# A hybrid decoder layer on one core: the merge's sums moved from GpSimd to VectorE, and four smaller moves in the order of loads and splits

## The reference

```python
h = _half_ffn(h, ffn1_pre_g, ffn1_w_gate, ffn1_w_up, ffn1_w_down, ffn1_post_g)
u = _rmsnorm(h, mix_pre_g)
c_q, c_kv, k_rope_raw, xb, yb, gate_mla, gate_lru = split(u @ w_in)
o_mla = _mla_branch(c_q, c_kv, k_rope_raw, ...)   # 8 heads, causal, then @ w_o_mla
o_lru = _rglru_branch(xb, yb, ...)                # conv, gated recurrence, then @ w_o_lru
merged = sigmoid(gate_mla) * o_mla + sigmoid(gate_lru) * o_lru
h = h + _rmsnorm(merged @ w_out, mix_post_g)
h = _half_ffn(h, ffn2_pre_g, ffn2_w_gate, ffn2_w_up, ffn2_w_down, ffn2_post_g)
```

## Time and profile before

| | |
|---|---|
| median of 3 runs | 2362.24 us (2359.62 to 2364.76) |
| profiled execution, its own time | 2362.34 us |
| its span in the trace | 2360.6 us |
| mean granted clock of TensorE | 0.975 of full |
| TensorE busy | 2217.9 us, 94% of the span |
| VectorE busy | 1242.3 us, 53% |
| ScalarE busy | 954.4 us, 40% |
| GpSimd busy | 350.7 us, 15% |

### The profile page before, as it was taken

The page is one execution under the profiler, slowest core; times in us unless marked ns, Lnnn a source line. Parts: engine busy times, 40 slices in busy tenths (PEclk is TensorE's granted clock), DMA queues, the critical chain, the costliest instruction groups (busy, mean ns, idle before and its releaser), DMA issues.

```text
span 2360.6 us, 26136 instructions
## 1 busy us (share of the span) xinstructions
PE 2217.9 (94%) x10101; PEld 1839.7 (78%) x10101; DVE 1242.3 (53%) x1596; ACT 954.4 (40%) x1529; POOL 350.7 (15%) x377
## 2 busy tenths in 40 slices
PE   4999999999998999999997888978699999999997
PEld 3888888888887888888986777856588888888886
DVE  7556655433636665212114887757755555543444
ACT  5333333332434767212324666434433333332332
POOL 5000000000402222000013555424300000000020
PEclk8999999999999999999998999989799999999999
DMA  3222222164442111223211002344122222235342
GB/s 116 72 72 64 80 71 72 56 215 149 134 136 65 52 50 47 72 76 115 69 36 36 8 10 80 121 166 165 62 72 63 72 63 73 71 125 194 109 152 89
DMA packets 198596, 209.48 MB, mean 89 GB/s; under 512 B 22277, under 2 KB 159562, under 8 KB 198474
## 3 DMA queue, kind: packets, MB, share of 16 engines
q1 hardware_dynamic: 198474, 207.81, 27.5%
HBM read 174.75 MB, written 32.51 MB: 88 GB/s over the span
## 4 chain that ended last, share of the span: by engine, by line
PE 83%; DVE 7%; POOL 3%; issue 3%; ACT 3%; DMA 1%; SPq 0%; POOLq 0%; ACTq 0%; DVEq 0%
PE ps L88 27%; PE ps L89 27%; PE ps L90 27%; DVE u_lo L98 1%; PE ps L1955 1%; PE ps L1987 1%; DVE w_lo L98 1%; POOL a_rot L1872 1%; ACT a_probs L1931 1%; PE ps L357 1%; DVE entry_y L342 1%; DVE ff_t L98 0%; DVE a_s L1921 0%; ACT entry_squares L282 0%; DVE a_pt L98 0%
## 5 line engine op out<-in xcount | busy, mean ns | idle before, releaser
L98 DVE TENSOR_TENSOR w_lo<-w_raw,w_hi 128x1024 fp32r<-128x1024 f32 (+3 forms) x169 | 205.1, 1217 | 282.2 <-ACT w_hi L94 281.8
L88 PE MATMUL ps<-ff_t,ff_w_hi 128*128 128x512 f32 x704 | 275.2, 391 | 15.8 <-DVE ff_t L98 15.8
L98 DVE TENSOR_TENSOR ff_w_lo<-ff_raw,ff_w_hi 128x512 fp32r<-128x512 f32 x264 | 182.9, 694 | 191.5 <-ACT ff_w_hi L94 191.3
L89 PE MATMUL ps<-ff_t,ff_w_hi 128*128 128x512 f32 x704 | 274.9, 390 | 0.0
L90 PE MATMUL ps<-ff_t,ff_w_lo 128*128 128x512 f32 x704 | 274.8, 390 | 0.0
L88 PE MATMUL ps<-w_hi,ff_hs 128*128 128x512 f32 x672 | 262.0, 390 | 6.4 <-DVE ff_hs L98 6.4
L90 PE MATMUL ps<-w_hi,ff_hs 128*128 128x512 f32 x672 | 261.5, 389 | 0.0
L89 PE MATMUL ps<-w_lo,ff_hs 128*128 128x512 f32 x672 | 261.4, 389 | 0.0
L94 ACT ACTIVATE w_hi<-w_raw 128x1024 fp32r<-128x1024 f32 (+3 forms) x169 | 169.7, 1009 | 187.4 <-PE ps L90 151.5
L94 ACT ACTIVATE ff_w_hi<-ff_raw 128x512 fp32r<-128x512 f32 x264 | 165.0, 628 | 184.5 <-PE ps L90 178.9
L88 PE MATMUL ps<-ff_b,ff_w_hi 128*128 128x512 f32 x528 | 207.8, 394 | 9.9 <-issue 8.3
(11 more groups left out here) (277 smaller groups left out, 4098.9 us busy)
## 6 DMA issues: line engine op xcount, KB each, us to landing
w_raw<-in_ffn_w_down_dram SPq DMA_DIRECT2D x88, 512.0 KB, 3.5
ff_raw<-in_ffn_w_gate_dram SPq DMA_DIRECT2D x44, 512.0 KB, 3.8
ff_raw<-in_ffn_w_up_dram SPq DMA_DIRECT2D x44, 512.0 KB, 3.9
w_raw<-in_w_in_dram SPq DMA_DIRECT2D x32, 512.0 KB, 3.9
w_raw<-in_w_out_dram SPq DMA_DIRECT2D x24, 512.0 KB, 4.2
spill_scratch<-ff_st SPq DMA_DIRECT2D x44, 256.0 KB, 2.9
ff_h<-spill_scratch SPq DMA_DIRECT2D x4, 2048.0 KB, 9.9
entry_x<-in_x_dram SPq DMA_DIRECT2D x8, 512.0 KB, 6.9
```

The lines of the kernel that those rows point to most:

```text
L88: pe.matmul(out, lh, rh, start=start, stop=False, skip_group_check=go_on)
L89: pe.matmul(out, lh, rl, start=False, stop=False, skip_group_check=go_on)
L98: return nc.vector.tensor_tensor(lo, src, as_f32(hi), ALU.subtract)
```

## The change

Four edits:

1. `am.add` runs on VectorE, right behind the product of the same block. Its wait for the landed transfers goes, since the product has made it.
2. SyncE issues w_out's load i = 7 ahead of the wait for the merge's end. Then come the norm's first gain and its first input row; the second gain stands behind load 8, and the other three input rows behind loads 9, 10 and 11.
3. The weights of the fourth head (`att.n_a[3]`) are loaded ahead of the rotary key's copies, and split in the attention's third step and no longer ahead of the first.
4. V tiles 4 and 5 are split ahead of the last tile's columns, and VectorE's `swap` comes behind `units[2]`.

```diff
--- before.py
+++ after.py
@@ -2122,11 +2122,10 @@
         dve.wait_ge(self.S["m_hi"], d + 1)
         split_lo(self.nc, self.c.u_lo[:, d, :], self.sum[:, d % 2, :], self.c.u_hi[:, d, :]).then_inc(self.S["m_split"], 1)
 
-    def add(self, pool, d):
-        pool.wait_ge(self.S["prod_done"], d + 1)
-        pool.wait_ge(self.landed[d % 5], 32 * (d // 5 + 1))
+    def add(self, dve, d):
+        dve.wait_ge(self.S["prod_done"], d + 1)
         x = self.sum[:, d % 2, :]
-        self.nc.gpsimd.tensor_tensor(x, x, self.other[d % 5], ALU.add).then_inc(self.S["add_done"], 1)
+        self.nc.vector.tensor_tensor(x, x, self.other[d % 5], ALU.add).then_inc(self.S["add_done"], 1)
 
     def branch_of(self, pe, d, chunks):
         c, att = self.c, self.att
@@ -2426,8 +2425,9 @@
                         lat.store(sp, 6)
                         lat.store(sp, 7)
                         break
+                w.load(sp, att.n_a[3])
                 att.key_rope_copy(sp)
-                for n in att.n_a[3:] + am.n[0:5]:
+                for n in att.n_a[4:] + am.n[0:5]:
                     w.load(sp, n)
                 for d in range(5):
                     am.load(sp, d)
@@ -2436,14 +2436,16 @@
                     am.load(sp, d)
                 for i in range(24):
                     w.load(sp, op.n[i // 8][i % 8])
-                    if i == 6:
+                    if i == 7:
                         sp.wait_ge(am.S["m_split"], DK)
                         sp.wait_ge(att.S["t_done"], HEADS * HEAD_PIECES)
                         sp.wait_ge(att.S["o_split"], 5)
                         gain(entry.post_gain, a["mix_post_g"][0])
+                        mid2.load(sp, 0)
+                    if i == 8:
                         gain(entry.pre_gain, a["ffn2_pre_g"][0])
-                        for t in range(4):
-                            mid2.load(sp, t)
+                    if i in (9, 10, 11):
+                        mid2.load(sp, i - 8)
                     if i == 13:
                         mid2.store(sp, 0)
                         mid2.store(sp, 1)
@@ -2564,19 +2566,19 @@
                 att.v_hi(act, 3)
                 att.rope_act(act, units[0])
                 att.unit_act(act, units[1])
+                att.v_hi(act, 4)
+                att.v_hi(act, 5)
                 lat.columns_hi(act, NT - 1)
-                for t in range(4, NT - 1):
-                    att.v_hi(act, t)
+                att.v_hi(act, 6)
                 att.unit_act(act, units[2])
                 att.v_last_hi(act)
                 att.unit_act(act, units[3])
                 att.rope_act(act, units[2])
                 att.key_rope_hi(act, 1)
                 w.hi(act, att.n_a[2])
-                w.hi(act, att.n_a[3])
                 for n in range(last_step + 2):
                     att.act_step(act, n)
-                    if n % HEAD_TILES == 2 and 0 < n // HEAD_TILES < HEADS:
+                    if n % HEAD_TILES == 2 and n // HEAD_TILES < HEADS:
                         w.hi(act, heads[n // HEAD_TILES + 3])
                 att.take(act, HEADS - 1, 1)
                 att.pair_hi(act, 3, half_of(1), 2 * HEADS)
@@ -2655,8 +2657,6 @@
                 att.rope_pool(pool, units[2])
                 for n in range(last_step):
                     att.pool_step(pool, n)
-                for d in range(DK):
-                    am.add(pool, d)
                 for g in range(1, 3):
                     for k in range(DK):
                         for s, q in out_steps(g, k):
@@ -2759,26 +2759,27 @@
                 att.v_lo(dve, 3)
                 att.rope_dve(dve, units[0])
                 att.unit_dve(dve, units[1])
+                att.v_lo(dve, 4)
+                att.v_lo(dve, 5)
                 lat.columns_lo(dve, NT - 1)
+                att.v_lo(dve, 6)
+                att.unit_dve(dve, units[2])
                 lat.swap(dve, 1)
-                for t in range(4, NT - 1):
-                    att.v_lo(dve, t)
-                att.unit_dve(dve, units[2])
                 att.v_lo(dve, NT - 1)
                 att.unit_dve(dve, units[3])
                 att.rope_dve(dve, units[2])
                 att.key_rope_lo(dve, 1)
                 w.lo(dve, att.n_a[2])
-                w.lo(dve, att.n_a[3])
                 for n in range(last_step + 2):
                     att.dve_step(dve, n)
-                    if n % HEAD_TILES == 2 and 0 < n // HEAD_TILES < HEADS:
+                    if n % HEAD_TILES == 2 and n // HEAD_TILES < HEADS:
                         w.lo(dve, heads[n // HEAD_TILES + 3])
                 att.add(dve, HEADS - 1, 1)
                 att.pair_lo(dve, 3, half_of(1), 5)
 
                 for d in range(DK):
                     am.product(dve, d)
+                    am.add(dve, d)
                     w.lo(dve, outs[d + 3])
                     if d > 0:
                         am.merged_lo(dve, d - 1)
```

## The result

| | before | after |
|---|---|---|
| median of 4 runs | 2362.30 us | 2341.34 us (2338.76 to 2343.29) |
| ratio, 95% interval | | 0.9911 (0.9894 to 0.9928) |
| profiled execution, its span | 2362.34, 2360.6 us | 2340.64, 2338.5 us |
| mean granted clock of TensorE | 0.975 | 0.982 |

The change takes 21.0 us off the kernel. 2336.6 us was forecast, with a range of 2331 to 2346, so the sign and the range held, and the forecast is 4.7 us too low. Run once more beside the experiments, the same program had a median of 2338.96 us against 2362.71: 23.8 us.

A forecast was written before the change was run, and what follows sets the result against it. Most of the chain is TensorE, so only stretches where it stands still can give time. Attention's start -10.2 and merge with output projection -15.5 sum to -25.7 us from 2362.34, giving 2336.6 us, range 2331 to 2346.

The forecast's parts named there:

- (a): Attention's start: V tiles split sooner; query unit at 1268.5 instead of 1271.12, VectorE begins on it 4.3 us earlier.
- (b): Attention's start: the later swap delays GpSimd's two rotary sums; third head's split at 1278.0, 1.3 us given back.
- rival 1: Attention's start: rotary chain and a dropping clock cost another 5 us, total 2341.8 us; chance 0.10.
- (c): Attention's start: fourth head's weights loaded earlier; first maximum at 1278.8 and exponential at 1279.9, 10.1 to 10.2 us sooner.
- (d): Attention's first scores: TensorE may keep the upper clock level; gain bounded at 2.5 us, taken as 0.
- rival 4: Attention's first steps: the clock stays up, total 2334 us; counted inside the main forecast's 0.82 chance.
- (e): Merge: sums on VectorE, u_lo 3.42 to 1.23 us, turn 5.3 to 4.3 or 4.9; TensorE waits 0.6 us at branch 3.
- (f): Output projection's start: the 2.70 us wait for the third chunk goes; last pair wanted at 1549.9.
- Rival 2: Merge: u_lo stays at 3.42 us, merge gives +1.5 instead of -15.5, total 2353.6 us; chance 0.05.
- (g): Output projection: last chunk's earlier load removes the 7.57 us wait; pair 13.2 us earlier, plus 2.3 us from full clock.
- (h): Output projection's second group: input rows and second gain between chunks 8 to 11 are covered; taken as 0, bounds 0 and 3 us.
- Rival 3: Output projection: loads and input rows queue at whole landing times, +7.9 us, total 2370.2 us; chance 0.02.

The follow-up runs named there:

- e7_only_loads: Kernel before with only the second edit (w_out load i = 7 issued ahead of gains and input rows): 2351.05 us, 0.9960 of before.
- e8: Kernel before with only the first edit (merge sums on VectorE instead of GpSimd): 2354.48 us, 0.9974 of before.
- e3: Changed kernel with the third edit undone (fourth head's weights loaded behind the key's copies, split ahead of the first maximum): 2348.38 us, 0.9939 of before.
- e4: Changed kernel with the fourth edit undone (V tiles 4 and 5 split behind the last columns and the swap): 2339.53 us, 0.9901 of before.
- e5: Changed kernel with VectorE's swap one place earlier, ahead of the second half's query unit: 2336.63 us, 0.9896 of before.
- e9: Changed kernel measured once more, as it is: 2338.96 us, 0.9902 of before.
- e1: Changed kernel with the first edit undone (merge sums back on GpSimd): 2347.00 us, 0.9929 of before.
- e6: Changed kernel with input rows 1 to 3 behind w_out loads 10, 11 and 12 instead of 9, 10 and 11: 2337.47 us, 0.9901 of before.

## Why the prediction held, and what it missed

(a) *V tiles.* The unit was put at 7.0 us after the last transposition, and it starts at 7.05. The 1.7 us of idle time came as 1.46, and the unit ran at full clock (0.227 us a pass from 1269.43 on). VectorE begins it at 1271.45, 9.4 us after the transposition, where 9.1 was forecast. What was not seen is that the kernel before is not always as slow here as in its one profile. Eight of the nine passes of its unit ran at half clock (1271.12 to 1274.52, about 0.43 us each); in e7_only_loads, with the same instructions up to here and 3.76 us of waiting, the clock came back within the unit's first pass. In e7 and e8 the exponential stands at 26.29 and 26.66, not at 28.05. Against these two the attention's part is worth 7.7 to 8.0 us. Of the other 1.4 to 1.8 us, 1.2 to 1.5 are the slower clock in that one profile (VectorE begins on the unit 13.45 us after the transposition, and 11.97 and 12.23 in e7 and e8); the rest is ScalarE's longer wait for the transfer (6.89 us against 6.62 and 6.73). Undone one at a time, the transfer is worth 7.5 us (e3) and V tiles with the swap 0.9 (e4).

(b) *The swap, 1.3 us given back: this term was mis-sized.* The swap came at 1273.61, the two GpSimd sums ended at 1277.36 and the third head's split began at 1279.37, 17.3 us after the transposition in place of the 16.5 forecast. With the swap early the exponential comes 1.9 us sooner (e5), so 1.9 us is what was given back, 0.6 more than the step had; 0.3 us came late from (a). The step let GpSimd's sum start where the swap ends, and it starts 0.43 us later (1274.30 to 1274.73); the rest is in the two sums, 2.63 us in place of 2.5. The error is of rival 1's kind, but that rival had another 5 us.

(c) *Head 4.* ScalarE waits for no transfer, and the maximum starts 0.85 us after the split, at 1280.22, sooner than the 1281 that was named as a sign of being wrong. The step has the exponential follow the maximum alone. What it left out is ScalarE's table load: it begins at 1279.41, ends at 1280.69, and the exponential starts 0.02 us behind it, also in e5, where the load waits 0.22 us for the split of the key's rotary part (1279.54 to 1280.82, exponential 1280.83). So by these rows a shorter `w_lo` of the third head on VectorE would alone gain nothing there. The displaced split, 0.56 us at 1286.57, cost nothing that can be seen: head 0 from its first exponential to the mask of step 8 took 18.2 us here and 19.3 in e9, against 19.0 and 19.2 in e7 and e8, which lack that split. TensorE was busy with the scores in front of it. The exponential was forecast 10.1 us sooner and came 9.4 sooner.

(d) *Clock, taken as 0.* The scores began at the upper level after 2.50 us of idle time (0.89 from 1280 to 1284), fell to 0.50 from 1284 to 1288 and were at 0.76 to 1292; before, 0.51 held from 1290 to 1302. From the first exponential to the mask of step 8 the head took 18.2 us (19.3 before, and 19.3 again in e9), so 0 was nearly right, and rival 4 did not come.

(e), (f) *The sums.* `u_lo` was priced at 1.23 us and is 1.22; the wait at branch 3 was put at 0.6 and is 0.46; the 2.70 us are gone. Rival 2 is dead by the after trace and by e1 and e8 from both sides. Of the two rules that the prediction weighed from the Trainium skill, the one of "SBUF — State Buffer", section Who interferes with whom, decides: the pair of two-input instructions on VectorE and GpSimd cost VectorE 2.2 us a time. The one of "Perfetto Trace Analysis", section Optimizing Scalar/DVE Operations, speaks for leaving sums on GpSimd when VectorE is saturated, though it adds that the two share a read port and that the offload might then not help. By e1 having the sums on GpSimd costs 6.7 us here, although VectorE was the busier engine. The rows of the kernel before show how, GpSimd's timeline first and then VectorE's:

```profile
1512.65 2.77 POOL L2129 TENSOR_TENSOR b_sum<-b_sum,b_in 128x1024 f32<-128x1024 f32 x1 [2.52 <-DVE b_sum L2118]
```

```profile
1513.09 3.42 DVE L98 TENSOR_TENSOR u_lo<-b_sum,u_hi 128x1024 fp32r<-128x1024 f32 x1
```

The sum begins first and ends at 1515.42, and `u_lo` ends 1.09 us behind it, nearly the whole of its own 1.22 us. In the four turns that follow it is 1.08 to 1.09 us again. So `u_lo` as good as stands until the sum is done, and the profile counts that as busy: VectorE is busy for 12.65 us with 7 instructions from 1520 to 1533 before, and for 12.63 us with 12 of them from 1513 to 1526 after.

The turns came as priced, 4.35 and then 4.89 us between products (4.3 and 4.9 in (e)). That each product would wait for TensorE did not come: VectorE runs behind TensorE and catches up, and of the eight products only the first and the last (0.65 us) wait. TensorE has no wait either but the 0.46 us, so the term was right all the same.

(g) *The load.* From the first merge product to the last pair it was 59.8 us (1503.24 to 1563.07) and is 46.8 (1496.30 to 1543.09): 13.0 sooner where 13.2 was forecast. From the pair's start to the wait for the evacuation it was 10.8 us and is 8.4, at 1.00 in place of 0.50: 2.4 where 2.3 was forecast. By the trace's own time the pair came 20.0 us sooner, not some 23: the attention gave less and heads 1 to 7 took back 2.9.

(h) *Five places, taken as 0: it cost 0.8.* TensorE's wait for the evacuation grew from 0.90 to 1.72 us (2.42 in e9), and e6 takes it back. Behind it 0.5 us came back in this profile (16.0 us from there to the norm's first transposition, 16.5 before), so that the merge gives 13.0 + 2.4 - 0.8 + 0.5 = 15.1. The cause is in ScalarE's order: it stands at a chunk of the second group until 1550.12, and the evacuation of the first group's rows is queued behind that split; VectorE's half of it, for which TensorE waits, stands in the same way behind the chunk's lower half.

```profile
1550.12 1.06 ACT L94 ACTIVATE w_hi<-w_raw 128x1024 fp32r<-128x1024 f32 x1 [0.90 <-DMA w_raw<-in_w_out_dram]
1551.09 1.06 ACT L2178 ACTIVATE entry_y<-ps 128x512 f32<-128x512 f32 x2
```

The cover that (h) named, 4.1 us of TensorE's work a chunk, was there for TensorE; what the step left out is who else waits behind ScalarE's wait. Rival 3, in which transfers take turns at their whole landing times (10.2 us a pair), is dead: DMA moved 350 to 400 GB/s from 1540 to 1555, and TensorE waited for no chunk of that group but the last pair, 0.51 us at 1581.45, as before (0.49). In e9, where ScalarE waits for three loads of the group in a row, they come 2.5 us apart (1544.33, 1546.90, 1549.42), each with an input row or gain issued between, so a pair costs less than the 3.5 us of (h).

*The sum.* -9.4 and -15.1 against -10.2 and -15.5: 1.2 us is what the steps got wrong, 0.8 in the attention and 0.4 in the merge. The other 3.5 us of the miss are no step of the prediction: 2.9 in heads 1 to 7, -0.5 in the rest of the span, 0.4 outside it (2340.64 less 2338.5 against 2362.34 less 2360.6), and 0.7 by which the median lies above the profiled execution. Heads 1 to 7 have the same instructions throughout; their stretches at the lower clock had fallen elsewhere. These windows cover that part, in the profile of before, of after and of e8_only_merge:

```profile
1309.00:1483.00 174.00, 151.35 (x867) 125.98 (x866) 142.24 (x225) 116.53 (x254) 91.58 (x125) 0.97 0.12 41
```

```profile
1299.00:1476.00 177.00, 153.26 (x868) 127.18 (x868) 142.12 (x225) 116.65 (x254) 91.66 (x125) 0.96 0.12 41
```

```profile
1308.00:1481.00 173.00, 148.99 (x869) 123.81 (x868) 142.12 (x225) 116.79 (x254) 91.64 (x125) 0.99 0.12 41
```

VectorE, ScalarE and GpSimd are busy for the same time in all three; TensorE is busy for 149.0 to 153.3 us as PEclk goes from 0.99 to 0.96. In the second comparison the heads took 174.0 and the change gave 23.8 us. With the heads at 173.7 us as before, the first measurement would have been about 2 us off the forecast and not 4.7. Why the clock falls in one place in one execution and in another in the next was not tried, and stays open.

## What to carry to other kernels

Ask of every wait who stands behind the waiting instruction on its own engine: that is where two of the four edits gave time (a load behind a wait for something else, a first exponential behind a transfer that it doesn't need), and where the one unforeseen cost came up. Here work of two SBUF inputs that alternated between VectorE and GpSimd on the same tiles was dearer than the same work on VectorE alone, by 6.2 to 6.7 us for eight sums, though VectorE counted as nearly full (busy for 12.65 of 13.00 us): look at what runs on the two at once before moving work to GpSimd. When several things are moved at once, undo them one by one: here half of one edit ate most of its other half, and the total doesn't show it.

## What the runs showed of the hardware that was not expected

- VectorE and GpSimd stretch each other in small operations too, and not always the same one loses. The swap, 0.69 us with GpSimd idle, took 1.25 us in e5, where it began 0.58 us into a GpSimd product of 1.29 us. In e4 the swap began 0.14 us before that product; it kept its 0.69 us and the product took 1.68 us in place of 1.28. Each time the one that began first kept its time. The merge of the kernel before shows the same: GpSimd's sum takes 2.77 us where VectorE's `w_lo` of 0.69 us began 0.17 us ahead of it, and 3.30 us where that `w_lo` is one of 1.22 us, and `u_lo`, which begins later, pays.
- The same idle time is answered by the clock differently from one execution to the next. After 3.75 to 3.80 us of waiting at the seventh V tile the lower level lasted through most of the unit in one trace (before), two to three passes of it in another (e8_only_merge) and about one in e7_only_loads and e4_undo_vtiles. Between before and e7_only_loads, which are alike up to there, the first exponential moved by 1.8 us.
- One and the same program for heads 1 to 7 took 172.6 to 176.6 us in twelve profiles. A single profile's span can't carry a claim of less than some 4 us; stages cut at fixed instructions can, where they leave that stretch out.
